# Two one-hots and two products of a step each in one VectorE instruction, the products behind the next step's one-hots

## Chip, cores and metric

One Trainium2 chip, one of its cores. The metric is the device time of the program in microseconds (us). The engines are PE (TensorE, with its weight loads as PEld), DVE (VectorE), ACT (ScalarE), POOL (GpSimd) and SP (SyncE, which issues DMAs).

## The reference, cut to what matters

One layer of a backbone over 1152 tokens (9 tiles of 128): modulation, a combined input projection, latent attention and retention, an output projection, and then an expert retrieval with product keys ("peer"). For each token and each of 8 heads the 16 best of 16384 = 128 x 128 experts are chosen; an expert's index is i * 128 + j.

```python
def peer(h, w_pq, sub_keys1, sub_keys2, u_table, v_table):
    ...
        cidx = (i1[..., :, None] * N_KEYS + i2[..., None, :]).reshape(PEER_BLOCK, PEER_HEADS, PEER_TOPK * PEER_TOPK)
        top_s, sel = lax.top_k(cand, PEER_TOPK)
        eidx = jnp.take_along_axis(cidx, sel, axis=-1)
        g = jax.nn.softmax(top_s, axis=-1).astype(xb.dtype)
        act = jax.nn.gelu(jnp.einsum('thkd,td->thk', u_table[eidx], xb), approximate=False)
        return jnp.einsum('thk,thkd->td', g * act, v_table[eidx])
```

## The kernel before, in words

The program is a row of stages with a barrier of all engines between them. Two of them matter here, `stage_weights` and the last, `stage_experts`.

The expert layer treats three of the nine token tiles sparsely (gathered rows of the tables) and six densely (768 tokens, in two groups of 384): there every expert's activation is computed for every token, and multiplied by that token's weight for that expert, which is zero for most. So for each dense token a 128 x 128 table of weights, W[i, j], is needed. It is made by a matmul: the partition is one of the token's 128 chosen (head, rank) pairs, the stationary operand is a one-hot of the pair's i over 128 keys, the moving one a one-hot of its j multiplied by the pair's share. The share is split into two float16 parts, so there are two matmuls a token, added in PSUM.

The class `WeightSteps` (L1705) holds this. A step covers B = 4 tokens; a group of 384 tokens has STEPS = 96 steps; a block of 16 tokens is stored to DRAM as a whole. Its methods:

- `vector` (L1734, DVE): a step's four instructions, all of 128 x 512 float16 (128 keys x 4 tokens). L1740 compares the key numbers (`iota`) with the pairs' j, giving `hot_j`; L1741 the same with i, giving `hot_i`; L1744 twice, `hot_j` times each part of the share, giving two `hot_w`. The buffers come in twos, by the parity `s` of the step. The columns of a step are four neighbouring tokens of the index (or share) table, repeated over the 128 keys by a stride of zero in the middle dimension; the four tokens are innermost and adjacent.
- `tensor` (L1747, PE): 8 matmuls of 128 x 128 (L1752) into a PSUM tile.
- `scalar` (L1756, ACT): evicts 128 x 512 values from PSUM (L1760).
- `store` (L1763, SP or POOL): writes a block to DRAM.

What orders a step are semaphores. `pw_full` starts at 2 (PE adds 2 at its start) and PE adds 1 at the end of each step. So DVE's wait for `pw_full >= n + 1` ahead of step n's first comparison means that the matmuls of step n - 2 are over; they were the last to read the buffers of that parity. `equal_full` counts the j comparisons, and the products wait for n + 1 of them. `hot_full` counts the finished products; PE waits for n + 1 ahead of step n. `pw_read` is what ACT has read (it starts at the number of PSUM buffers, here 2).

In `stage_weights` (L1770) the first group's 96 steps are made with nothing beside them. Ahead of the steps PE transposes the hidden rows of the three sparse tiles into `p_h` (L1825), and ACT reads them (L1835). `steps` unrolls the steps 0 and 1 and runs the others in a hardware loop (Fori) of two steps a turn, on DVE, PE and ACT alike. SP stores the 24 blocks.

In `stage_experts` (L1848) a group's 128 turns each go through one block of 128 experts: `down` and `up` matmuls of PE (L2124, L2125, L2128, L2144), the splits of the tables into two parts by ACT (L1976 `u_hi`, L1981 `v_hi`) and DVE (L2041 `u_lo`, L2048 `v_lo`), the activation by ACT (L1986) and, on DVE, the product with the weight (L2054) and its split (L2057, L2059), and the sparse tiles' three dot products or sums (L2066, L2079). In the first 96 turns of the first group the second group's weights are made on the way, one step a turn (`weights` in `blocks`): DVE's four instructions stand between `u_lo` and L2054, with their own buffers (named `next_`) and one PSUM buffer. DVE's part of this stage is written out, not looped.

One line elsewhere serves as a measure: L1640 (`stage_scores`) compares 16-bit values in a `tensor_tensor` of 128 x 2048, seen as 8 x 16 x 16 a partition, whose first operand is broadcast along the innermost dimension.

Of the kernel before, what the change touches and what calls it, by code (L numbers as in the profile page):

```python
# [10 lines left out]
F16 = mybir.dt.float16  # L11
ALU = mybir.AluOpType
# [3 lines left out]
P = 128  # L16
# [18 lines left out]
N_KEYS = 128  # L35
# [57 lines left out]
class Links:  # L93


    def __init__(self, eng, sem):
        self.eng, self.sem, self.base, self.n = eng, sem, 0, 0
# [939 lines left out]
def wait_count(eng, sem, count):  # L1037

    if not isinstance(count, int) or count > 0:
        eng.wait_ge(sem, count)  # L1040
# [664 lines left out]
class WeightSteps:  # L1705
# [5 lines left out]
    B = 4  # L1711
# [3 lines left out]
    def __init__(self, nc, sem, m, keep, banks, name, base, iota):  # L1715

        B = self.B
        self.nc, self.keep, self.banks, self.base = nc, keep, banks, base
        self.hot_i = [m.sb(f"{name}_hot_i{i}", [P, N_KEYS, B], F16) for i in range(2)]
        self.hot_j = [m.sb(f"{name}_hot_j{i}", [P, N_KEYS, B], F16) for i in range(2)]  # L1720
        self.hot_w = [[m.sb(f"{name}_hot_w{i}{k}", [P, N_KEYS, B], F16) for k in range(2)] for i in range(2)]
        self.iota = iota.rearrange("p (k b) -> p k b", b=B)
        self.wt = m.sb(f"{name}_wt", [P, 2, N_KEYS, BLOCK])
        self.pw = [m.ps(f"{name}_pw{i}", [P, B, N_KEYS]) for i in range(banks)]
        self.iota_full, self.equal_full, self.hot_full, self.pw_full, self.pw_read, self.wt_free, self.stored = (
            sem(f"{name}_{x}") for x in ("iota_full", "equal_full", "hot_full", "pw_full", "pw_read", "wt_free", "w_stored"))

    def keys(self, dve):
# [2 lines left out]
        self.nc.vector.tensor_copy(self.iota, src).then_inc(self.iota_full, 1)  # L1731
        dve.wait_ge(self.iota_full, 1)

    def vector(self, dve, n, s):  # L1734

        nc, keep = self.nc, self.keep
        shape = [P, N_KEYS, self.B]
        column = lambda x: x[:, bass.ds(n * self.B + self.base, self.B)].unsqueeze(1).to_broadcast(shape)
        dve.wait_ge(self.pw_full, n + 1)
        nc.vector.tensor_tensor(self.hot_j[s][:], self.iota, column(keep.index[:, 1]), ALU.is_equal).then_inc(self.equal_full, 1)  # L1740
        nc.vector.tensor_tensor(self.hot_i[s][:], self.iota, column(keep.index[:, 0]), ALU.is_equal)  # L1741
        dve.wait_ge(self.equal_full, n + 1)
        for k in range(2):
            last = nc.vector.tensor_tensor(self.hot_w[s][k][:], self.hot_j[s][:], column(keep.parts[:, k]), ALU.mult)  # L1744
        last.then_inc(self.hot_full, 1)

    def tensor(self, pe, n, s):  # L1747
        pe.wait_ge(self.hot_full, n + 1)
        pe.wait_ge(self.pw_read, n + 1)
        for b in range(self.B):  # L1750
            for k in range(2):
                last = self.nc.tensor.matmul(self.pw[s % self.banks][:, b, :], self.hot_i[s][:, :, b], self.hot_w[s][k][:, :, b],  # L1752
                                             start=k == 0, stop=k == 1)
        last.then_inc(self.pw_full, 1)

# [14 lines left out]
def stage_weights(nc, sem, m, keep, a):  # L1770

    iota = m.sb("iota", [P, N_KEYS * WeightSteps.B], F16)
    w = WeightSteps(nc, sem, m, keep, 2, "first", 0, iota[:])
    BLOCKS = w.STEPS // w.PER_BLOCK
    rest = m.sb("w_rest", [P, DENSE])
    hs = [m.sb(f"h_cols{s}", [P, KD, P]) for s in range(SPARSE)]
    p_idx = m.ps("p_idx", [P, 3, 512])
    p_h = m.ps("p_h", [P, KD, P])
    h_in = [sem(f"h_cols_in{s}") for s in range(SPARSE)]
    part_done, idx_full, idx_done, rows_full, rows_read = (  # L1780
        sem(x) for x in ("part_done", "idx_full", "idx_done", "h_rows_full", "h_rows_read"))

    def steps(eng, body):
        body(0, 0)
        body(1, 1)
        with eng.Fori(1, w.STEPS // 2) as k:
            for s in range(2):
                body(k * 2 + s, s)

    with nc.Block() as block:  # L1790

        @block.vector
        def _(dve):
            def link(ins, n):
                ins.then_inc(part_done, 1)
                dve.wait_ge(part_done, n)

            w.keys(dve)
            shares = keep.pairsT[:, 2, DENSE_AT:T]
            nc.vector.tensor_copy(keep.index, keep.pairsT[:, 0:2, DENSE_AT:T])  # L1800
            link(nc.vector.tensor_scalar(rest[:], shares, SHARE_UNIT, None, ALU.mult), 1)
            link(nc.vector.tensor_copy(keep.parts[:, 0, :], rest[:]), 2)
            link(nc.vector.tensor_sub(rest[:], rest[:], keep.parts[:, 0, :]), 3)
            link(nc.vector.tensor_copy(keep.parts[:, 1, :], rest[:]), 4)
            dve.wait_ge(idx_full, 1)
            tiles = lambda r: p_idx[:, r, 0:DENSE_AT].rearrange("p (s k) -> p s k", s=SPARSE)
            nc.vector.tensor_copy(keep.shares, tiles(2))
            nc.vector.tensor_copy(keep.dots, tiles(0)).then_inc(idx_done, 1)
            dve.wait_ge(idx_done, 1)
            nc.vector.scalar_tensor_tensor(out=keep.experts.bitcast(U32), in0=tiles(1), scalar=float(N_KEYS), in1=keep.dots,  # L1810
                                           op0=ALU.mult, op1=ALU.add).then_inc(idx_done, 1)
            steps(dve, lambda n, s: w.vector(dve, n, s))

        @block.tensor
        def _(pe):
            pe.sem_inc(w.pw_full, 2)
            for r in range(3):
                for s in range(SPARSE):
                    last = nc.tensor.transpose(p_idx[:, r, s * P:(s + 1) * P], keep.pairsT[:, r, s * P:(s + 1) * P], keep.ident)
            last.then_inc(idx_full, 1)  # L1820
            for s in range(SPARSE):
                pe.wait_ge(h_in[s], 16)
                wait_count(pe, rows_read, s)
                for k in range(KD):
                    last = nc.tensor.transpose(p_h[:, k, :], hs[s][:, k, :], keep.ident)  # L1825
                last.then_inc(rows_full, 1)
            steps(pe, lambda n, s: w.tensor(pe, n, s))

        @block.scalar
        def _(act):  # L1830
            act.sem_inc(w.wt_free, 1)
            act.sem_inc(w.pw_read, w.banks)
            for s in range(SPARSE):
                act.wait_ge(rows_full, s + 1)
                nc.scalar.activation(keep.h_rows[:, s, :], p_h[:].rearrange("p k c -> p (k c)"), ACT.Copy).then_inc(rows_read, 1)  # L1835
            steps(act, lambda n, s: w.scalar(act, n, s))

        @block.sync
        def _(sp):
            for s in range(SPARSE):  # L1840
                sp.dma_start(hs[s][:], keep.h2_dram[:, :, s * P:(s + 1) * P]).then_inc(h_in[s], 16)
            w.store(sp, 0)
            with sp.Fori(1, BLOCKS) as b:
                w.store(sp, b)
            sp.wait_ge(w.stored, 16 * BLOCKS)
# [430 lines left out]
```

## Time and profile before

| | us |
|---|---|
| median of 3 runs | 4201.07 (4199.33 to 4202.46) |
| the profiled execution | 4197.49 |
| its span, first to last instruction | 4195.7 |
| PE busy | 3802.9 (91%) |
| DVE busy | 2992.6 (71%) |
| ACT busy | 1232.7 (29%) |
| POOL busy | 1747.3 (42%) |
| mean granted PE clock | 0.932 |

The profile is one execution, taken by the hardware profiler. The steps of `stage_weights` run from about 1776 to 1917 us of the span; `stage_experts` begins at 1922 and ends with the kernel. A row of a timeline gives the start, the length, the engine, the line, the operation, output and inputs by the program's names, the shape and the number of instructions merged into the row; in brackets, how long the engine was idle before and whom it waited for. PEclk is the granted PE clock as a share of 2.4 GHz. A DVE instruction can begin before the one ahead of it has ended.

### The profile page before, as it was taken

How to read it: one execution, taken by the hardware profiler on the slowest of the kernel's cores; microseconds unless marked ns; L12 is line 12 of the kernel's file. 1: busy time of each engine (PE TensorE's matmuls, PEld its weight loads, DVE VectorE, ACT ScalarE, POOL GpSimd, SP SyncE). 2: the span in 40 equal slices, each digit the busy share in tenths (PEclk: the TensorE clock that was granted, in tenths of full speed). 3: DMA queues.
4: the chain of work that ended last, by engine and by line, in shares of the span. 5: the costliest groups of instructions: out<-in, count | busy, mean ns of one | idle time of the engine just before them, and what ended most of it. 6: DMA issues, size and time to landing. Idle time of an engine off the chain costs nothing.

```text
span 4195.7 us, 58772 instructions
## 1 busy us (share of the span) xinstructions
PE 3802.9 (91%) x19146; PEld 3082.0 (73%) x19146; DVE 2992.6 (71%) x6028; ACT 1232.7 (29%) x1871; POOL 1747.3 (42%) x1065
## 2 busy tenths in 40 slices
PE   8899876999668999387999999999989999999998
PEld 1699843566555444166999999999979999999997
DVE  0322244333441999897999999998888888888888
ACT  0411033222222222074333333333223232332332
POOL 0222000000220233202565565555557777777775
PEclk9799977899779999657999999999999999999999
DMA  7388700566433111047999999999999999999997
GB/s 248 114 269 286 250 2 20 161 202 205 139 111 97 35 35 35 15 180 278 328 339 333 327 339 327 346 327 354 336 336 338 343 333 345 336 341 345 331 347 273
DMA packets 302319, 1018.03 MB, mean 243 GB/s; under 512 B 30394, under 2 KB 61916, under 8 KB 294932
## 3 DMA queue, kind: packets, MB, share of 16 engines
q1 hardware_dynamic: 155348, 489.04, 34.8%
q0 software_dynamic: 127584, 481.35, 31.5%
q10 hardware_dynamic: 19296, 46.67, 2.9%
q8 instruction: 28, 0.46, 0.0%
q14 instruction: 63, 0.52, 0.0%
HBM read 875.22 MB, written 141.72 MB: 242 GB/s over the span
## 4 chain that ended last, share of the span: by engine, by line
PE 52%; DVE 1%; DMA 0%; issue 0%; ACT 0%; DVEq 0%; POOLq 0%
PE p_y L2144 25%; PE p_a L2125 9%; PE p_a L2124 9%; PE p_a L2128 8%; PE next_pw L1752 2%; DMA h_lo<-h_spill 0%; DVE p_y L2110 0%; DVE h_lo L2096 0%; DVE rows L2066 0%; DVE h_rows L2079 0%; DVE h_rows L2102 0%; DVE h_hi L2094 0%; DVE x1g L2113 0%; ACT pairsT L1986 0%; DVE u_raw L2105 0%
## 5 line engine op out<-in xcount | busy, mean ns | idle before, releaser
L2013 POOL DMA_INDIRECT rows<-in_v,pairsT x384 | 763.2, 1987 | 276.3 <-DVE h_rows L2079 184.4
L2013 POOL DMA_INDIRECT rows<-u_rows,pairsT x384 | 632.9, 1648 | 477.0 <-DVE pairsT L2066 404.5
L2124 PE MATMUL p_a<-h_hi,u_hi 128*128 128x384 f32 x2048 | 688.7, 336 | 39.3 <-DVE h_lo L2096 38.0
L2125 PE MATMUL p_a<-h_lo,u_hi 128*128 128x384 f32 x2048 | 692.1, 338 | 0.0
L2144 PE MATMUL p_y<-v_hi,g_hi 128*128 128x512 f32 x1536 | 486.9, 398 | 0.0
L1981 ACT ACTIVATE v_hi<-v_raw 128x1024 fp32r<-128x1024 f32 x256 | 272.0, 1062 | 727.0 <-PE p_y L2144 714.1
L2144 PE MATMUL p_y<-v_lo,g_hi 128*128 128x512 f32 x1536 | 475.8, 391 | 0.0
L2079 DVE SCALAR_TENSOR_TENSOR h_rows<-rows,pairsT,h_rows 128x1024 f32<-128x1024 f32 x381 | 466.4, 1279 | 2.1 <-DMA rows<-in_v,pairsT 2.1
L2066 DVE CUSTOM_DVE_ANT_0 rows<-rows,h_rows 128x1024 f32<-128x1024 f32 x384 | 450.6, 1220 | 24.1 <-DMA rows<-u_rows,pairsT 23.9
L2124 PEld LDWEIGHTS p_a<-h_hi,u_hi 128*128 128x128 f32 x2048 | 386.2, 189 | 50.4 <-DVE h_lo L2096 38.7
L2128 PE MATMUL p_a<-h_hi,u_lo 128*128 128x384 f32 x2048 | 396.8, 334 | 0.5 <-DVE u_lo L2041 0.5
L2125 PEld LDWEIGHTS p_a<-h_lo,u_hi 128*128 128x128 f32 x2048 | 385.9, 188 | 9.8
L2144 PE MATMUL p_y<-v_hi,g_lo 128*128 128x512 f32 x1536 | 389.7, 389 | 0.0
L2128 PEld LDWEIGHTS p_a<-h_hi,u_lo 128*128 128x128 f32 x2048 | 358.6, 188 | 0.8 <-DVE u_lo L2041 0.8
L2041 DVE TENSOR_TENSOR u_lo<-u_raw,u_hi 128x1024 fp32r<-128x1024 f32 x256 | 312.4, 1220 | 48.8 <-ACT u_hi L1976 47.5
L2144 PEld LDWEIGHTS p_y<-v_lo,g_hi 128*128 128x128 f32 x1536 | 288.3, 188 | 65.5
L2144 PEld LDWEIGHTS p_y<-v_hi,g_lo 128*128 128x128 f32 x1536 | 288.3, 188 | 59.9
L2144 PEld LDWEIGHTS p_y<-v_hi,g_hi 128*128 128x128 f32 x1536 | 281.0, 189 | 43.2
L2048 DVE TENSOR_TENSOR v_lo<-v_raw,v_hi 128x1024 fp32r<-128x1024 f32 x256 | 312.2, 1219 | 0.0
L1976 ACT ACTIVATE u_hi<-u_raw 128x1024 fp32r<-128x1024 f32 x256 | 270.1, 1055 | 14.8 <-DMA u_raw<-in_uT 14.8
L1478 PE MATMUL psc<-wc,hs 128*128 128x512 f32 x576 | 251.6, 595 | 0.0
L466 DVE COPY pairsT<-pT 128x1024 f32<-128x1024 f32 x64 | 78.3, 1224 | 232.8 <-DMA u_rows<-pairsT 143.6
(301 smaller groups left out, 5806.4 us busy)
## 6 DMA issues: line engine op xcount, KB each, us to landing
u_raw<-in_uT SPq DMA_DIRECT2D x256, 512.0 KB
v_raw<-in_v SPq DMA_DIRECT2D x256, 512.0 KB
w_ring<-weights_spill POOLq DMA_DIRECT2D x32, 1536.0 KB
u_rows<-pairsT ACTq DMA_DIRECT2D x64, 512.0 KB
key_cols<-in_uT SPq DMA_DIRECT2D x64, 512.0 KB, 4.1
u_rows<-key_rows SPq DMA_DIRECT2D x64, 512.0 KB
wada<-in_w_ada SPq DMA_DIRECT2D x12, 2048.0 KB, 7.9
weights_spill<-first_wt SPq DMA_DIRECT2D x24, 1024.0 KB
```

What stands on the lines that cost most here:

```text
L1478: last = nc.tensor.matmul(psc[:, 4 * b:4 * b + 4, :], hs[:, k, :], wc[:, k, 4 * b:4 * b + 4, :], start=k == 0, stop=k == KD - 1)
L1976: nc.scalar.activation(u_hi[s][:], u_raw[s][:], ACT.Copy).then_inc(uhi_full, 1)
L1981: nc.scalar.activation(v_hi[s][:], v_raw[s][:], ACT.Copy).then_inc(vhi_full, 1)
L2013: pool.indirect_dma_start(rows[s][n % SLOTS][:], None, (keep.u_rows, v_rows)[g], at).then_inc(rows_in[s][n % SLOTS], 16)
L2041: nc.vector.tensor_sub(u_lo[s][:], u_raw[s][:], u_hi[s][:].bitcast(F32)).then_inc(ulo_full, 1)
L2048: nc.vector.tensor_sub(v_lo[s][:], v_raw[s][:], v_hi[s][:].bitcast(F32)).then_inc(vlo_full, 1)
L2066: nc.vector.tensor_tensor_reduce(out=slot[:], in0=slot[:], in1=keep.h_rows[:, s, :], op0=ALU.mult, op1=ALU.add, scale=1.0, scalar=0.0, acc ...
L2079: nc.vector.scalar_tensor_tensor(out=total, in0=slot[:], scalar=share, in1=total, op0=ALU.mult, op1=ALU.add).then_inc(rows_used, 1)
L2124: nc.tensor.matmul(p_a[:, 0:GT], u_hi[s][:, k, :], h_hi[:, k, :], start=k == 0, stop=False)
L2125: nc.tensor.matmul(p_a[:, 0:GT], u_hi[s][:, k, :], h_lo[:, k, :], start=False, stop=False)
L2128: last = nc.tensor.matmul(p_a[:, 0:GT], u_lo[s][:, k, :], h_hi[:, k, :], start=False, stop=k == KD - 1)
L2144: last = nc.tensor.matmul(p_y[i][:, half, :], part, vv[:, half * 512:(half + 1) * 512], start=first and hi and vv is v_hi[s], stop=end and ...
```

## The change

The two one-hots (i and j) become one tile `hot` of 128 x 2 x 128 x 4 float16, and the two products one tile `hot_w` of the same shape, each made by one instruction over 1024 elements a partition. `vector` is split into `equal` and `weighted`. `stage_experts` still calls `vector`, which issues the one behind the other. In `stage_weights` DVE's order is now: the one-hots of step n + 1, then the products of step n. The counts of the waits are the same functions of the step's number as before. PE's, ACT's and SP's code is the same but for the operands' names.

```diff
-        self.hot_i = [m.sb(f"{name}_hot_i{i}", [P, N_KEYS, B], F16) for i in range(2)]
-        self.hot_j = [m.sb(f"{name}_hot_j{i}", [P, N_KEYS, B], F16) for i in range(2)]
-        self.hot_w = [[m.sb(f"{name}_hot_w{i}{k}", [P, N_KEYS, B], F16) for k in range(2)] for i in range(2)]
+        self.hot = [m.sb(f"{name}_hot{i}", [P, 2, N_KEYS, B], F16) for i in range(2)]
+        self.hot_w = [m.sb(f"{name}_hot_w{i}", [P, 2, N_KEYS, B], F16) for i in range(2)]
...
+    def columns(self, x, n):
+
+        return x[:, :, bass.ds(n * self.B + self.base, self.B)].unsqueeze(2).to_broadcast([P, 2, N_KEYS, self.B])
+
+    def equal(self, dve, n, s):
+
+        dve.wait_ge(self.pw_full, n + 1)
+        keys = self.iota.unsqueeze(1).to_broadcast([P, 2, N_KEYS, self.B])
+        self.nc.vector.tensor_tensor(self.hot[s][:], keys, self.columns(self.keep.index, n), ALU.is_equal).then_inc(self.equal_full, 1)
+
+    def weighted(self, dve, n, s):
+
+        dve.wait_ge(self.equal_full, n + 1)
+        hot_j = self.hot[s][:, 1].unsqueeze(1).to_broadcast([P, 2, N_KEYS, self.B])
+        self.nc.vector.tensor_tensor(self.hot_w[s][:], hot_j, self.columns(self.keep.parts, n), ALU.mult).then_inc(self.hot_full, 1)
+
     def vector(self, dve, n, s):
...
-        dve.wait_ge(self.pw_full, n + 1)
-        nc.vector.tensor_tensor(self.hot_j[s][:], self.iota, column(keep.index[:, 1]), ALU.is_equal).then_inc(self.equal_full, 1)
-        nc.vector.tensor_tensor(self.hot_i[s][:], self.iota, column(keep.index[:, 0]), ALU.is_equal)
-        dve.wait_ge(self.equal_full, n + 1)
-        for k in range(2):
-            last = nc.vector.tensor_tensor(self.hot_w[s][k][:], self.hot_j[s][:], column(keep.parts[:, k]), ALU.mult)
-        last.then_inc(self.hot_full, 1)
+        self.equal(dve, n, s)
+        self.weighted(dve, n, s)
...
-                last = self.nc.tensor.matmul(self.pw[s % self.banks][:, b, :], self.hot_i[s][:, :, b], self.hot_w[s][k][:, :, b],
+                last = self.nc.tensor.matmul(self.pw[s % self.banks][:, b, :], self.hot[s][:, 0, :, b], self.hot_w[s][:, k, :, b],
...
-            steps(dve, lambda n, s: w.vector(dve, n, s))
+            def step(n, s):
+                w.equal(dve, n + 1, 1 - s)
+                w.weighted(dve, n, s)
+
+            w.equal(dve, 0, 0)
+            step(0, 0)
+            step(1, 1)
+            with dve.Fori(1, w.STEPS // 2 - 1) as k:
+                for s in range(2):
+                    step(k * 2 + s, s)
+            step(w.STEPS - 2, 0)
+            w.weighted(dve, w.STEPS - 1, 1)
```

## Rows read from the trace of the kernel before

**Rows 1.** The page: busy time of each engine.
```profile
PE 3802.9 (91%) x19146; PEld 3082.0 (73%) x19146; DVE 2992.6 (71%) x6028; ACT 1232.7 (29%) x1871; POOL 1747.3 (42%) x1065
```

**Rows 2.** Windows of the weights stage and of the expert stage; columns on top.
```profile
core 0: us, PE busy (x) PEld busy (x) DVE busy (x) ACT busy (x) POOL busy (x), PEclk, DMA share, GB/s
...
1800.00:1900.00 100.00, 80.56 (x582) 60.30 (x583) 100.00 (x291) 78.14 (x73) 0.00 (x0) 0.50 0.46 189
...
1948.00:2840.00 892.00, 892.00 (x4826) 806.42 (x4825) 826.21 (x1441) 324.66 (x383) 517.36 (x325) 1.00 0.93 332
```

**Rows 3.** Timeline of the weights stage's first steps.
```profile
1783.09 1.99 PEld L1752 LDWEIGHTS first_pw<-first_hot_w,first_hot_i 128*128 128x128 f16 x16
1783.30 2.07 PE L1752 MATMUL first_pw<-first_hot_w,first_hot_i 128*128 128x128 f16 x16
...
1784.60 0.43 DVE L1740 TENSOR_TENSOR first_hot_j<-iota,gate 128x512 f16<-128x512 f16 x1 [5.56 <-PE first_pw L1752]
...
1786.09 1.11 PE L1752 MATMUL first_pw<-first_hot_w,first_hot_i 128*128 128x128 f16 x8 [0.72 <-DVE first_hot_w L1744]
...
1787.36 0.42 DVE L1740 TENSOR_TENSOR first_hot_j<-iota,gate 128x512 f16<-128x512 f16 x1
1787.43 1.11 PE L1752 MATMUL first_pw<-first_hot_w,first_hot_i 128*128 128x128 f16 x8 [0.23 <-DVE first_hot_w L1744]
...
1787.70 0.42 DVE L1741 TENSOR_TENSOR first_hot_i<-iota,gate 128x512 f16<-128x512 f16 x1
1788.04 0.75 DVE L1744 TENSOR_TENSOR first_hot_w<-first_hot_j,gate 128x512 f16<-128x512 f16 x2
1788.71 0.43 DVE L1740 TENSOR_TENSOR first_hot_j<-iota,gate 128x512 f16<-128x512 f16 x1
...
1788.85 1.12 PE L1752 MATMUL first_pw<-first_hot_w,first_hot_i 128*128 128x128 f16 x8 [0.30 <-DVE first_hot_w L1744]
```

**Rows 4.** Timeline of the weights stage's last steps and the next stage's start.
```profile
1911.73 1.11 PE L1752 MATMUL first_pw<-first_hot_w,first_hot_i 128*128 128x128 f16 x8 [0.26 <-DVE first_hot_w L1744]
...
1913.00 0.42 DVE L1740 TENSOR_TENSOR first_hot_j<-iota,gate 128x512 f16<-128x512 f16 x1
...
1914.49 1.12 PE L1752 MATMUL first_pw<-first_hot_w,first_hot_i 128*128 128x128 f16 x8 [0.26 <-DVE first_hot_w L1744]
...
1921.98 0.35 SPq L1938 DMA_DIRECT2D u_raw<-in_uT  x1
```

**Rows 5.** Groups of DVE and ACT instructions, 1786 to 1913.
```profile
L1744 DVE TENSOR_TENSOR first_hot_w<-first_hot_j,gate 128x512 f16<-128x512 f16 x185 | 69.6, 417 | 0.0
L1740 DVE TENSOR_TENSOR first_hot_j<-iota,gate 128x512 f16<-128x512 f16 x92 | 39.0, 424 | 0.0
...
L1760 ACT ACTIVATE first_wt<-first_pw 128x512 f32 (+1 forms) x92 | 99.1, 1077 | 28.3 <-PE first_pw L1752 21.8 <-SPq L1765 3.4 <-issue 3.2
```

**Rows 6.** Instructions of line 1740: the register work ahead of the comparison.
```profile
L1740 DVEq FUSED_REGOPS  x94: 75/75/81, 1784.5 to 1912.9; - x94
```

**Rows 7.** Timeline of DVE in one weighted turn of the expert stage.
```profile
2056.97 1.22 DVE L2041 TENSOR_TENSOR u_lo<-u_raw,u_hi 128x1024 fp32r<-128x1024 f32 x1
2058.11 0.42 DVE L1740 TENSOR_TENSOR next_hot_j<-pairsT,gate 128x512 f16<-128x512 f16 x1
...
2059.45 0.55 DVE L2054 TENSOR_TENSOR pairsT<-pairsT,w_ring 128x384 f32<-128x384 f32 x1
2060.04 0.36 DVE L2057 CAST g_hi<-pairsT 128x384 fp32r<-128x384 f32 x1
```

**Rows 8.** Waits between 1948 and 2840: us in total, times, longest.
```profile
DVE u_lo L2041 <- ACT u_hi L1976: 42.5, 69, 0.7
```

**Rows 9.** Groups of DVE instructions, whole span: another 16-bit tensor_tensor with a broadcast.
```profile
L1640 DVE TENSOR_TENSOR mix<-sel_abf,starts 128x2048 bf16<-128x2048 bf16 x9 | 20.6, 2292 | 0.3
L1640 DVE TENSOR_TENSOR mix<-sel_abf,iota 128x2048 bf16<-128x2048 bf16 x9 | 20.6, 2284 | 0.0
```

More of the change, by code:

```diff
@@ L1732, in keys @@
         dve.wait_ge(self.iota_full, 1)
-    def vector(self, dve, n, s):
-        nc, keep = self.nc, self.keep
-        shape = [P, N_KEYS, self.B]
-        column = lambda x: x[:, bass.ds(n * self.B + self.base, self.B)].unsqueeze(1).to_broadcast(shape)
-        dve.wait_ge(self.pw_full, n + 1)
-        nc.vector.tensor_tensor(self.hot_j[s][:], self.iota, column(keep.index[:, 1]), ALU.is_equal).then_inc(self.equal_full, 1)
-        nc.vector.tensor_tensor(self.hot_i[s][:], self.iota, column(keep.index[:, 0]), ALU.is_equal)
-        dve.wait_ge(self.equal_full, n + 1)
-        for k in range(2):
-            last = nc.vector.tensor_tensor(self.hot_w[s][k][:], self.hot_j[s][:], column(keep.parts[:, k]), ALU.mult)
-        last.then_inc(self.hot_full, 1)
+    def columns(self, x, n):
[8 more added lines that the diff above has]
+        self.nc.vector.tensor_tensor(self.hot_w[s][:], hot_j, self.columns(self.keep.parts, n), ALU.mult).then_inc(self.hot_full, 1)
+    def vector(self, dve, n, s):
+        self.equal(dve, n, s)
+        self.weighted(dve, n, s)
     def tensor(self, pe, n, s):
```

## The prediction

> **What bounds the kernel now.** I read the page first, to see how much of the span belongs to the code touched, then each of the two stages that use it, by windows, by groups of instructions and as a timeline. The page says that PE is busy 91% and DVE 71% [rows 1]. That is a mean over stages. The windows part two stages from each other [rows 2]: in the expert stage (1948 to 2840, while it still makes weights) PE has no idle time at the full clock; in the weights stage (1800 to 1900) DVE reads 100.00 of 100 us, PE 80.56 and ACT 78.14, at a granted clock of 0.50, the 1.2 GHz level.
>
> *The weights stage.* DVE at 100% looks like a DVE bound, and the change looks like fewer instructions for the bound engine. The timeline says more. Call the n-th group of matmuls PE(n). PE(2) starts at 1786.09 and the equality of step 4 at 1787.36; PE(93) starts at 1911.73 and the equality of step 95 at 1913.00: 1.27 us both times [rows 3, 4]. Step 5's is at 1788.71, 1.28 after PE(3) at 1787.43. Never earlier, at either end of the stage. So the wait on `pw_full` is binding: each equality starts when PE has finished the step two before (1.11 us of matmuls, then some 0.16 for the semaphore and DVE's 75 ns of register work [rows 6]). From the first equality of a step to the end of its last product is 0.68 + 0.75 = 1.43 us (1787.36, 1788.04, length 0.75), and PE starts 0.06 later (1788.79 to 1788.85) [rows 3]. The loop PE(n-2), DVE(n), PE(n) is 1.275 + 1.43 + 0.06 = 2.765 us and spans two steps: 1.382 a step. Measured: from step 2's equality at 1784.60 to step 95's at 1913.00, 128.40 / 93 = 1.381. The instructions of 417 to 424 ns start every 0.33 us and so overlap [rows 3, 5], which is why a loop through a semaphore shows as a DVE without idle time. Two loops interleave, one for even steps and one for odd; DVE needs 4 x 0.333 = 1.33 itself, almost as much.
>
> *The expert stage.* A weighted turn takes about 9.25 us, PE filled. DVE is busy 826.21 of 892 us, so has 65.8 / 96 = 0.69 us a turn to spare [rows 2], and waits 42.5 us there for ACT's `u_hi` [rows 8].
>
> **The change, part by part.**
>
> *1. Two instructions for four.* A 16-bit 128x512 lasts 0.417 and starts 0.333 after the one before [rows 3, 5]; a 32-bit 128x1024 lasts 1.22 and is followed 1.14 later (2056.97, 2058.11) [rows 7]. Against the 0.55 of 384 elements (L2054) [rows 7] the latter gives (1.22 - 0.55) / 640 = 1.05 ns an element and a fixed 0.15 of length. Taking the same 0.15 off 0.417 leaves 0.267 for 512 elements, 0.52 ns each, and so 0.067 fixed between starts. So 1024 16-bit elements at the present pace cost 0.533 + 0.067 = 0.60 between starts and 0.683 in length (estimates). Bounds: between starts at least 0.53 (no fixed part), at most 0.667 (nothing saved); length 0.62 to 0.75 (the pair now). I take 0.60 and 0.683. Gain on DVE alone: 1.333 - 1.20 = 0.13 us a step.
>
> The far bound is another pace altogether. L1640, a 16-bit tensor_tensor of 2048 with a broadcast operand and more dimensions, lasts 2284 to 2292 ns, twice our time per element [rows 9]. There the broadcast repeats one element innermost; here the innermost run remains four neighbouring tokens, as it is now, and only an outer dimension of 2 is added, so I take the fast pace. The Trainium skill has the rule, in "VectorE: DVE Perf Modes", What auto-detection actually checks: two results a cycle if every tensor is 16-bit with innermost step 1. By that rule too the merged instruction keeps the pace, and L1640 agrees with it.
>
> *2. The order.* This is the term that matters. The semaphore starts at 2 and PE(n) makes it n + 3. The equality of step m waits for m + 1, hence for PE(m-2). Before, what stood ahead of it on DVE was the products of m-1, and PE(m-2) needs only those of m-2: one whole step of slack. Now `step(n)` issues the equality of m = n + 1 and then the products of n. The equality of n + 1 waits for PE(n-1), which waits for the products of n-1, **the instruction directly ahead of that equality on DVE**. Queued behind the waiting equality are the products of n, for which PE(n) waits. So nothing overlaps any more: products(n-1), PE(n-1), equality(n+1), products(n), PE(n). One period is now one step:
> 1.275 (start of PE(n-1) to the equality) + 0.60 (to the products) + 0.683 (their length) + 0.06 (to PE(n)) = 2.62 us.
> The wait of the products for their own equality is met long before and costs nothing; the cover is the other equality and a whole PE step.
>
> *3. The stage.* PE(0) is held until 1783.09 by the transposes of `p_h`, not by DVE, and stays at 1783.30 [rows 3]. Equality 2 stays at 1784.60; the products of step 1 are now behind it and end at 1784.60 + 0.60 + 0.68 = 1785.88; PE(1) at 1785.94. PE(94) 93 periods later: 1785.94 + 93 x 2.62 = 2029.6. The last products wait for nothing, so PE(95) follows after a plain PE step, at least 7 x 0.117 and about 1.0: 2030.6. Before it was at 1914.49 [rows 4]. Difference: **+116 us**. ACT's step (1.08 us) and the stores of four steps' results each fit into 2.62 and 10.5 us; from the last matmul to the next stage at 1921.98 is as before. The clock is at 0.50 already [rows 2], and a PE with more idle time has no lower level to fall to.
>
> *4. The expert stage.* Here `vector` is the equality and the products with nothing between. The products now wait for an instruction just issued. The nearest row: L2054, 0.55 long, is followed by its dependent L2057 after 0.59 (2059.45, 2060.04) [rows 7], so a dependent start costs the length plus 0.04. DVE's step: 0.683 + 0.04 + 0.60 = 1.32 against 1.34 now (2058.11 to 2059.45). Even were the gap 0.2 us longer, the 0.69 of slack a turn covers it, and PE sets the end: 0. If that cover were gone, each 0.1 us would cost 96 x 0.1 = 9.6 us.
>
> *Sum.* The profiled execution's 4197.5 us becomes 4313.5. It lies 3.6 below the median of the runs, 4201.07; on that scale: **4317 us**, 2.8% slower.
> Bounds: a period of 1.27 + 0.53 + 0.62 + 0.05 = 2.47 gives 93 x 2.47 - 127.5 = +102; 1.28 + 0.667 + 0.75 + 0.06 = 2.76 gives +129. That is 4303 to 4330, and some us either way for what else shifts.
>
> **The rivals.**
>
> *A. The merged instructions lose the fast pace.* Against it: the innermost run is unchanged. For it: L1640 shows that such an instruction can run at half the pace. Then between starts 1.14, length 1.22: period 1.275 + 1.14 + 1.22 + 0.06 = 3.70, and 93 x 1.08 = 100 us more. In the expert stage DVE's step would be 1.26 + 1.14 = 2.40, 1.06 over now, 0.37 over the slack, so DVE would set the turn: 96 x 0.37 = 36 us. Together 4317 + 100 + 36 = 4453. If only one of the two loses it, about half.
>
> *B. Faster: the wait does not bite and the saved fixed costs remain.* It would need equality n + 1 to be released by PE(n-2), at the place of the `pw_full` wait in the loop. Then DVE alone sets the step, at 1.20: 93 x (1.20 - 1.381) = -17 us, 4184. It decides as soon as PE's answer returns within the 0.60 us of one products instruction; the rows say 1.27, and it starts only when they are done, so it cannot. The Trainium skill speaks for this side: "VectorE: DVE Perf Modes", Rules for kernel authors, advises to keep the number of DVE operations small rather than that of semaphores, since the flush behind each one comes anyway. The fixed 0.067 us of fixed time between starts bears that out for DVE alone; that rule looks at one engine, and would turn this forecast's sign.
>
> *C. No change: the added wait is absorbed by a stall that I do not see*, so that the merged pair and the lost overlap cancel. There is no idle time of 1.2 us a step anywhere in rows 2 to 5 to absorb it. 4201.
>
> **How the numbers follow.** The forecast has 0.90: the count of the semaphore is plain in the code and the loop's latency is a row at both ends of the stage. A has 0.06, B 0.03, C 0.01. What a measurement of this kernel tells from no change is about 0.2%, 8.4 us. Slower is forecast and A, 0.96; faster is B, 0.03; same C, 0.01. The rivals lie far from the forecast and hold 0.10, so the range stays with the forecast's own bounds, 4303 to 4330, widened a little for the scatter of runs (3 us) and for second-order shifts: 4300 to 4336.
>
> **What would show it.** In the profile after: the weights stage ends near 2038 in place of 1922; DVE has two groups of 96 instructions of about 0.68 us there, and idle time of about 1.3 us ahead of each equality, put down to PE `first_pw`; PE idle about 1.5 us a step, put down to DVE; PE(n) starts 2.6 us apart; busy DVE in 1800 to 1900 falls from 100% to about 50%. The expert stage keeps its 9.25 us turns and its length. Wrong would be: instructions of 1.2 us (A), periods near 1.2 to 1.4 us with no idle DVE (B), or an expert stage longer by over 5 us, which would mean that DVE's slack there was not the cover I take it for.

## The result and the profile after

The changed kernel takes 4315.77 us (median of 4 runs, 4312.65 to 4318.72) against 4201.76 before it on the same chip: a ratio of 1.0272, 95% interval 1.0254 to 1.029, so slower by 114 us. The profiled execution has a span of 4312.6 us, 116.9 more than the one before. Forecast were 4317 us and a range of 4300 to 4336.

Busy time of the engines, from the page:

```profile
PE 3802.1 (88%) x19146; PEld 3082.3 (71%) x19146; DVE 2979.8 (69%) x5644; ACT 1231.0 (29%) x1871; POOL 1735.1 (40%) x1065
```

No engine works noticeably more than in [rows 1] (PE's weight loads 0.3 us); DVE has 384 instructions and 12.8 us less. The added time is idle time. The windows say where; the first lies in the weights stage, the second is the expert stage's weighted part, moved by 116 us (columns on top):

```profile
core 0: us, PE busy (x) PEld busy (x) DVE busy (x) ACT busy (x) POOL busy (x), PEclk, DMA share, GB/s
...
1800.00:1900.00 100.00, 42.63 (x310) 31.97 (x309) 49.16 (x76) 40.10 (x38) 0.00 (x0) 0.50 0.23 94
...
2064.00:2956.00 892.00, 892.00 (x4826) 806.50 (x4825) 822.87 (x1249) 324.82 (x383) 518.08 (x324) 1.00 0.94 332
```

Against [rows 2], the expert stage is the same to the matmul: 4826 in 892 us, PE without a gap. In the weights stage 310 matmuls pass in 100 us where 582 did, and DVE falls from 100.00 to 49.16. Its timeline, the first steps and the last:

```profile
1784.14 1.13 PE L1759 MATMUL first_pw<-first_hot_w,first_hot 128*128 128x128 f16 x8
...
1785.31 0.69 DVE L1741 TENSOR_TENSOR first_hot<-iota,gate 128x1024 f16<-128x1024 f16 x1 [6.31 <-PE first_pw L1759]
...
1786.66 1.11 PE L1759 MATMUL first_pw<-first_hot_w,first_hot 128*128 128x128 f16 x8 [1.39 <-DVE first_hot_w L1747]
...
1787.94 0.69 DVE L1741 TENSOR_TENSOR first_hot<-iota,gate 128x1024 f16<-128x1024 f16 x1 [1.34 <-PE first_pw L1759]
1788.55 0.68 DVE L1747 TENSOR_TENSOR first_hot_w<-first_hot,gate 128x1024 f16<-128x1024 f16 x1
1789.29 0.83 PEld L1759 LDWEIGHTS first_pw<-first_hot_w,first_hot 128*128 128x128 f16 x8 [1.80 <-DVE first_hot_w L1747]
...
2030.32 2.06 PE L1759 MATMUL first_pw<-first_hot_w,first_hot 128*128 128x128 f16 x16 [1.39 <-DVE first_hot_w L1747]
...
2038.73 0.35 SPq L1956 DMA_DIRECT2D u_raw<-in_uT  x1
```

This is to be read in turns. PE(1) starts at 1786.66, the one-hots at 1787.94 (1.28 later), the products at 1788.55, PE(2) at 1789.29. DVE is idle for 1.34 us while PE works, and PE for about 1.5 while DVE works: "PE waits for DVE" and "DVE waits for PE" of similar size, in the same stretch, on the same pair of tiles, is the mark of a loop that is closed once a step. In [rows 3, 4] the same loop ran over two steps; once the stage was under way (from PE(3) on), DVE showed no wait there and PE one of 0.23 to 0.30 us. PE(94) starts at 2030.32, so the period is (2030.32 - 1786.66) / 93 = 2.620 us.

The waits between 1790 and 2030 (total, times, longest):

```profile
PE first_pw L1759 <- DVE first_hot_w L1747: 137.4, 91, 1.5
DVE first_hot L1741 <- PE first_pw L1759: 122.0, 92, 1.3
```

DVE in a weighted turn of the expert stage:

```profile
2173.35 0.68 DVE L1741 TENSOR_TENSOR next_hot<-pairsT,gate 128x1024 f16<-128x1024 f16 x1
2174.07 0.69 DVE L1747 TENSOR_TENSOR next_hot_w<-next_hot,gate 128x1024 f16<-128x1024 f16 x1
2174.68 0.55 DVE L2072 TENSOR_TENSOR pairsT<-pairsT,w_ring 128x384 f32<-128x384 f32 x1
```

The step takes 1.33 us, where it was 1.34 [rows 7]. From the stage's first DMA to the end are 4312.6 - 2038.73 = 2273.9 us; before, 4195.7 - 1921.98 = 2273.7.

### The profile page after: what moved, and what is told of

It is laid out like the page before. It is cut to its first block, busy times and chain, and to the rows that moved or that the text cites. A ratio compares the mean times of both kernels' runs of the same rounds, so it can differ in the third digit from the quotient of the medians.

```text
span 4312.6 us, 58192 instructions
## 1 busy us (share of the span) xinstructions
PE 3802.1 (88%) x19146; PEld 3082.3 (71%) x19146; DVE 2979.8 (69%) x5644; ACT 1231.0 (29%) x1871; POOL 1735.1 (40%) x1065
## 4 chain that ended last, share of the span: by engine, by line
PE 50%; DVE 1%; DMA 1%; issue 0%; POOL 0%; ACT 0%; ACTq 0%; DVEq 0%; POOLq 0%
PE p_y L2162 23%; PE p_a L2143 8%; PE p_a L2142 8%; PE p_a L2146 8%; PE next_pw L1759 2%; DMA rows<-u_rows,pairsT 1%; DMA h_lo<-h_spill 0%; DVE rows L2084 0%; DVE p_y L2128 0%; DVE h_lo L2114 0%; DVE h_rows L2097 0%; POOL rows L2031 0%; DVE h_rows L2120 0%; DVE h_hi L2112 0%; DVE x1g L2131 0%
## 5 line engine op out<-in xcount | busy, mean ns | idle before, releaser
L2031 POOL DMA_INDIRECT rows<-in_v,pairsT x384 | 750.3, 1954 | 288.2 <-DVE h_rows L2097 199.9
L2066 DVE TENSOR_TENSOR v_lo<-v_raw,v_hi 128x1024 fp32r<-128x1024 f32 x256 | 312.3, 1220 | 0.0
```

What stands on the lines that cost most here:

```text
L2031: pool.indirect_dma_start(rows[s][n % SLOTS][:], None, (keep.u_rows, v_rows)[g], at).then_inc(rows_in[s][n % SLOTS], 16)
L2066: nc.vector.tensor_sub(v_lo[s][:], v_raw[s][:], v_hi[s][:].bitcast(F32)).then_inc(vlo_full, 1)
```

## The experiments

The experiments ran on three chips, each beside the kernel before on the same chip (medians 4200.4, 4201.1 and 4201.2 us), to which the ratios refer. The total moves by a few us from run to run, so beside it stands a finer measure from the traces: the time from the first to the last weight load of PE in the weights stage. For the changed kernel (number: minimum/median/maximum length in ns, first and last start in us), and for the fastest version below:

```profile
L1759 PEld LDWEIGHTS first_pw<-first_hot_w,first_hot x768: 111/126/151, 1783.9 to 2032.0; 128*128 128x128 f16 x192
```

```profile
L1761 PEld LDWEIGHTS first_pw<-first_hot_w,first_hot x768: 111/125/151, 1784.5 to 1898.5; 128*128 128x128 f16 x192
```

| kernel | first to last load, us | median, us | ratio to before (95%) |
|---|---|---|---|
| before | 1783.1 to 1915.2: 132.1 | 4201 | |
| the change | 248.1 | 4315.8 | 1.0254 to 1.029 |
| merge only | 1783.9 to 1921.4: 137.5 | 4204.6 | 1.0000 to 1.0018 |
| order only | 1781.7 to 2043.5: 261.8 | 4330.6 | 1.0296 to 1.0328 |
| three one-hot buffers | 1788.4 to 1915.8: 127.4 | 4195.8 | 0.998 to 0.9998 |
| 4 one-hot, 3 product, 3 PSUM buffers | 114.0 | 4182.0 | 0.9941 to 0.9968 |
| the same, not merged | 1785.6 to 1912.2: 126.6 | 4196.0 | 0.9979 to 0.9997 |
| merge only, DVE written out | 1789.5 to 1917.2: 127.7 | 4195.7 | 0.9979 to 0.9997 |
| the change, DVE written out | 1784.4 to 2021.3: 236.9 | 4305.1 | 1.0237 to 1.0268 |
| the change, half of the stage's matmuls | 1784.9 to 1987.7: 202.8 | 4269.6 | 1.0148 to 1.0182 |
| before, half of the stage's matmuls | 1784.6 to 1912.1: 127.5 | 4195.0 | 0.9977 to 0.9997 |
| the change, one more comparison a weighted turn | 1782.9 to 2030.9: 248.0 | 4318.5 | 1.0264 to 1.0298 |
| the same, one token broadcast innermost | 1783.0 to 2031.0: 248.0 | 4366.2 | 1.038 to 1.0415 |

**Merge or order?** Two runs take the change apart. The first keeps the merged instructions and the old order:

```diff
-            w.equal(dve, 0, 0)
-            step(0, 0)
...
+            steps(dve, lambda n, s: w.vector(dve, n, s))
```

> The merged instructions in the old order: equality and products of step n, nothing between, also in the weights stage. Theory (the order is the cause, the merge costs nothing): the equality again follows PE(n-2). From its start to the end of the products 0.72 + 0.69 = 1.41 us (the merged rows of the changed kernel's expert stage: 2173.35, 2174.07), so two steps take 1.275 + 1.41 + 0.06 = 2.745 and one 1.37, against 1.381: about 1 us less in all, 4201 within 3 us. Rival (the merge is the cause, since PE must wait for one large product and the products for one large comparison): most of the 114 us stays, above 4260.

The second keeps the order and splits both instructions again:

```diff
+        for r in (1, 0):
+            at = self.keep.index[:, r, bass.ds(n * self.B + self.base, self.B)].unsqueeze(1).to_broadcast(shape)
+            last = self.nc.vector.tensor_tensor(self.hot[s][:, r], self.iota, at, ALU.is_equal)
...
+        for k in range(2):
...
+            last = self.nc.vector.tensor_tensor(self.hot_w[s][:, k], self.hot[s][:, 1], at, ALU.mult)
```

> The new order with four separate instructions of 512 elements (two comparisons, two products). Theory: the loop through PE is closed once a step, with DVE's part 1.43 us as in the kernel before: 1.275 + 1.43 + 0.06 = 2.765 us a step, 0.145 more than the changed kernel's 2.62, so 93 x 0.145 = 13 us above its 4316: 4329. Rival (the merge is the cause): near 4201.

Measured 4204.6 and 4330.6. The order is the cause: alone it costs 130 us, with the merge 114. The rival (above 4260, and near 4201) is out by 55 us in the one run and by 130 in the other. The order alone shows the same turns with a longer part of DVE: PE to PE 2.78 us, and the comparisons 1.30 after PE:

```profile
1851.01 1.12 PE L1765 MATMUL first_pw<-first_hot_w,first_hot 128*128 128x128 f16 x8 [1.65 <-DVE first_hot_w L1752]
1852.31 0.76 DVE L1743 TENSOR_TENSOR first_hot<-iota,gate 128x512 f16<-128x512 f16 x2 [1.36 <-PE first_pw L1765]
...
1853.79 1.11 PE L1765 MATMUL first_pw<-first_hot_w,first_hot 128*128 128x128 f16 x8 [1.67 <-DVE first_hot_w L1752]
```

But the merge alone is no gain either, 4 us worse where 1 better was expected. On the total alone that is barely told from no change (the interval begins at 1.0000); the stage says it more clearly, 137.5 us for 132.1. Its timeline:

```profile
1850.11 0.68 DVE L1741 TENSOR_TENSOR first_hot<-iota,gate 128x1024 f16<-128x1024 f16 x1
...
1850.25 1.11 PE L1759 MATMUL first_pw<-first_hot_w,first_hot 128*128 128x128 f16 x8 [0.32 <-DVE first_hot_w L1747]
...
1850.93 0.69 DVE L1747 TENSOR_TENSOR first_hot_w<-first_hot,gate 128x1024 f16<-128x1024 f16 x1
1851.54 0.69 DVE L1741 TENSOR_TENSOR first_hot<-iota,gate 128x1024 f16<-128x1024 f16 x1
```

The products start 0.82 us after their one-hots, not 0.72 as in the expert stage, whose DVE code is written out. DVE's own time is then 0.82 + 0.61 = 1.43 us a step, more than the 1.38 of the kernel before, and the saving of two instructions is gone. (The loop through PE over two steps has the gap in it too and gives nearly the same, (1.27 + 0.82 + 0.69 + 0.06) / 2 = 1.42.) With four small instructions another comparison, that of i, stood between the comparison of j and the products; with two large ones nothing stands there.

**Is that gap register work of the loop?** The same kernel, DVE's 96 steps written out:

```diff
-            steps(dve, lambda n, s: w.vector(dve, n, s))
+            for n in range(w.STEPS):
+                w.vector(dve, n, n % 2)
```

> The merged instructions in the old order, with DVE's 96 steps written out in place of its hardware loop (PE's and ACT's loops stay). In the looped version the products began 0.82 us after their one-hots, not 0.72, and DVE's own 0.82 + 0.61 = 1.43 us set the step. Theory: the 0.10 is register work that DVE's queue does only once the wait of the products is met, and it is gone here: DVE 0.72 + 0.61 = 1.33 us, the loop of two steps 1.20 + 1.41 + 0.06 = 2.67, so 1.34 a step, 93 x 0.10 = 9 us less than the looped version: 4196. Rival (the gap belongs to the dependent pair whatever the code around it): as the looped version, 4204.

```profile
1850.87 0.69 DVE L1741 TENSOR_TENSOR first_hot<-iota,gate 128x1024 f16<-128x1024 f16 x1
...
1851.60 0.69 DVE L1747 TENSOR_TENSOR first_hot_w<-first_hot,gate 128x1024 f16<-128x1024 f16 x1
1852.21 0.69 DVE L1741 TENSOR_TENSOR first_hot<-iota,gate 128x1024 f16<-128x1024 f16 x1
```

0.73 us, 1.34 a step, 4195.7: as expected. The unmerged kernel with DVE written out was not run, so how much of the 5 us under the kernel before is the merge's, and how much that of writing out, stays open. In the looped version this row (operation, times: min/median/max in ns) stands between the two, register work of DVE's queue that comes only when the wait is met (the last one-hots run from 1919.1 to 1919.8, this starts at 1919.8, the products at 1919.9). It is 0.06 of the 0.09 us; the rest is not resolved:

```profile
L1747 DVEq FUSED_REGOPS  x94: 57/57/57, 1786.2 to 1919.8; - x94
```

The changed kernel, written out in the same way (its `step` called for n from 0 to 94 in place of the loop):

> The changed kernel with DVE's steps of the weights stage written out. Theory: the answer of PE comes back as late as before, less the 57 to 75 ns of register work ahead of the one-hots: 2.62 - 0.07 = 2.55 us a step, 93 x 0.07 = 7 us less: 4309. The serial loop stays. Rival (what costs is the hardware loop on DVE): far less than 4290.

```profile
1852.12 1.11 PE L1759 MATMUL first_pw<-first_hot_w,first_hot 128*128 128x128 f16 x8 [1.39 <-DVE first_hot_w L1747]
1853.27 0.69 DVE L1741 TENSOR_TENSOR first_hot<-iota,gate 128x1024 f16<-128x1024 f16 x1 [1.21 <-PE first_pw L1759]
```

Measured 4305.1, 10.7 us less rather than 7. PE(n-1) to the one-hots are now 1.15 us in place of 1.27, so the loop form had cost 0.12 there, 0.07 of it the register row and the rest not resolved. The hardware loop adds to the serial period; it is not what makes it serial.

**Is PE's time wholly exposed?** Half of the weights stage's matmuls, those of the share's low part, are left out, in the changed kernel and in the one before:

```diff
+        parts = 1 if self.banks == 2 else 2
         for b in range(self.B):
-            for k in range(2):
+            for k in range(parts):
```

> The changed kernel with the second of each token's two matmuls left out in the weights stage (the share's low part is missing there). Theory: PE's step is wholly exposed in the loop, so a step of 4 matmuls less at 0.117 us each is 0.47 shorter, 2.15 us: 94 x 0.47 = 44 us off 4316, 4272. Rival (DVE or a store sets the step): no change, 4316.

> The kernel before with the same matmuls left out (the share's low part is missing in the weights stage). Theory: the loop over two steps shortens to 2.30 us, 1.15 a step, and DVE's four instructions take over at 1.33 to 1.36: 93 x 0.02 to 0.05 = 2 to 4 us off, about 4198. Were PE exposed as in the changed kernel, it would be 44 off; were DVE alone the bound, nothing.

Measured 4269.6 and 4195.0. The same 4 matmuls a step are worth 46 us in the changed kernel (first to last load 202.8 for 248.1) and 6 in the one before (127.5 for 132.1, its DVE at 1.34 us a step). In the order of before, PE's work lay beside DVE's; in the new one it is added to it.

**Do more buffers mend it?** A third one-hot buffer, with loops of six steps, lets the one-hots of n + 1 wait for PE(n-2):

```diff
-        dve.wait_ge(self.pw_full, n + 1)
+        s = s % self.hots
+        wait_count(dve, self.pw_full, n + 3 - self.hots)
```

> The change with a third buffer for the one-hots in the weights stage (loops of 6 steps a turn), so that the one-hots of step n + 1 wait for PE(n-2), as they did before the change. Theory: two steps a loop, 1.275 + 0.61 + 0.68 + 0.06 = 2.63 us, 1.31 a step, 93 x 0.07 = 6 us under the kernel before: 4195. The PSUM loop (1.46 from PE's start to ACT's, 1.07, back to PE) gives 1.29 a step, just under it. Rival (something else in the merged order costs time, the wait is only where it shows): stays above 4260.

> Four buffers for the one-hots, three for the products, three PSUM buffers in the weights stage (loops of 12 steps): the one-hots of n + 1 wait for PE(n-3). Theory: no loop through PE binds any more (three steps for 2.63 us) and DVE's own two instructions set the step, 0.61 + 0.61 = 1.22 us: 93 x 0.16 = 15 us under the kernel before, 4186. If ACT's eviction (1.07 and its wait) sets it instead: 1.30 or so a step, 4194.

> The version with four one-hot, three product and three PSUM buffers, in the new order, but with four separate instructions a step. It parts that version's 18 us into buffers and merge. Theory: no loop through PE binds, DVE's four instructions set the step at 1.33 us: 93 x 0.05 = 4 us under the kernel before, 4196, so that 4 come from the buffers and 13 from the merge, which only now is on the path. Rival (all of it is the buffers): 4182.

All three landed near their numbers: 4195.8, 4182.0 and 4196.0. The deeper set is 4 us under its number. With the third buffer, the order that cost 114 us costs nothing; the step is 127.4 / 95 = 1.34 us rather than 1.31. The longer loop turns that came with the buffer are not what undid it: with all steps written out and two buffers the change still takes 4305.1. The rows read as if ACT's way back bound beside DVE's:

```profile
1850.91 0.85 PEld L1761 LDWEIGHTS first_pw<-first_hot_w,first_hot 128*128 128x128 f16 x8 [0.43 <-DVE first_hot_w L1749]
...
1852.39 1.08 ACT L1769 ACTIVATE first_wt<-first_pw 128x512 f32 x1 [0.20 <-SPq L1774]
1852.80 0.68 DVE L1749 TENSOR_TENSOR first_hot_w<-first_hot,gate 128x1024 f16<-128x1024 f16 x1
...
1853.59 0.85 PEld L1761 LDWEIGHTS first_pw<-first_hot_w,first_hot 128*128 128x128 f16 x8 [0.44 <-DVE first_hot_w L1749]
```

ACT evicts the PE step of 1850.91 from 1852.39 to 1853.47, and PE's next load into that PSUM buffer is at 1853.59: a loop of 2.68 us over two steps, 1.34 a step. The products end at 1853.48, within 0.01 of ACT, and the profile puts PE's wait down to them. No run changes the PSUM buffers alone, so this cause is read and not shown. With the deeper set DVE waits for nobody (1800 to 1890) and goes without a gap at 0.60 us an instruction:

```profile
1879.82 0.68 DVE L1743 TENSOR_TENSOR first_hot<-iota,gate 128x1024 f16<-128x1024 f16 x1
1880.42 0.68 DVE L1749 TENSOR_TENSOR first_hot_w<-first_hot,gate 128x1024 f16<-128x1024 f16 x1
1881.03 0.68 DVE L1743 TENSOR_TENSOR first_hot<-iota,gate 128x1024 f16<-128x1024 f16 x1
```

Here the merge pays: unmerged, the same buffers give 126.6 us of stage, merged 114.0, 12.6 / 95 = 0.13 us a step, the figure that the saved fixed parts give. (In the serial loop the merge took 14 us off the stage too, 261.8 to 248.1, since there all of DVE's time counts; but that stage is twice as long.) Three kinds of buffers and the length of the loops' turns changed together here, and no run parts them. The deeper merged version is 18 us faster than the kernel before and 134 faster than the changed one.

**Is the expert stage's slack what it was taken for?** One more comparison a weighted turn, into a tile of its own, in the fast form and then with one token broadcast innermost:

```diff
...
+        at = self.keep.index[:, :, bass.ds(n * self.B + self.base, self.B)].unsqueeze(2).to_broadcast(whole)
+        self.nc.vector.tensor_tensor(self.extra[:], self.iota.unsqueeze(1).to_broadcast(whole), at, ALU.is_equal)
```

> The changed kernel with one more comparison of 1024 16-bit elements in each weighted turn of the expert stage (into a tile of its own): 0.61 us more for DVE, 96 times. Theory: DVE's slack there, (892 - 822.9) / 96 = 0.72 us a turn, still hides it: 4316 to 4320. Rival (DVE sets that stage's turn): 96 x 0.61 = 58 more, 4374.

> The same with the additional comparison's second operand broadcast innermost too (one token for all). Theory: that takes the slow pace of the kernel's other 16-bit comparison with such a broadcast, 1.22 us long, 1.14 between starts, 0.42 over the slack: 96 x 0.42 = 40 us more, 4356. If the pace stays at 0.61: as the run before it. If the slack is not what the windows say: between 4316 and 4426.

Measured 4318.5 and 4366.2. The added group of each, in turn:

```profile
L1755 DVE TENSOR_TENSOR next_extra<-pairsT,gate 128x1024 f16<-128x1024 f16 x96 | 66.0, 687 | 0.0
```

```profile
L1755 DVE TENSOR_TENSOR next_extra<-pairsT,gate 128x1024 f16<-128x1024 f16 x96 | 117.1, 1220 | 0.0
```

and two of the second one's waits between 2064 and 2956:

```profile
PEld next_pw L1764 <- DVE next_hot_w L1748: 44.8, 87, 0.6
PE next_pw L1764 <- DVE next_hot_w L1748: 17.3, 85, 0.3
```

The first is hidden whole (first to last `next_pw` load 879.1 us, as before). The second is not: 923.7 us, 44.7 more or 0.47 a turn, and PE now waits for the products. So 1.14 - 0.47 = 0.67 us a turn can be used, close to the 0.69 and 0.72 that the windows give; the total of 50 is 10 over what was expected, about half of it in these turns (44.7 for 40), the rest outside them and not explained. The two forms differ in one stride, and in length by 687 to 1220 ns.

## Why the prediction was right

- *The binding wait.* That the equality is always 1.27 to 1.28 us behind PE(n-2) was read as a loop at a time when DVE showed 100% busy. The pair with half of the matmuls bears it out from the other side: take PE's work away in the kernel before, and it goes to DVE's 1.34 us and no further.
- *Part 1, the two large instructions.* 0.60 between starts and 0.683 long were estimated; 0.61 and 0.684 to 0.692 measured. The fast pace holds with the additional outer dimension, so rival A is out. That a broadcast along the innermost dimension would have about halved it is shown by the second of the runs with an added comparison. The rule of the Trainium skill that the prediction cites ("VectorE: DVE Perf Modes", What auto-detection actually checks: two results a cycle if every tensor is 16-bit with innermost step 1) is borne out on both sides, 687 and 1220 ns.
- *Part 2, the order.* 2.62 us a step forecast, 2.620 measured. The pair of merge alone and order alone shows that the cause is the order, and the third buffer that it is the wait's distance within the order.
- *Part 3, the stage.* +116 forecast, +116.0 between first and last load, 116.9 in the span and 114 in the medians. Two small things that the sum left out offset each other on the scale of the runs: PE(0) came at 1784.14, 0.84 later than before through something in an earlier stage, and the profiled execution lay 1.4 us below its median, not 3.6. That part of the closeness is luck.
- *Part 4, the expert stage.* 1.32 forecast, 1.33 measured, hidden; the cover of 0.69 us a turn was 0.67.
- *Rival B, and the rule that spoke for it.* The advice of the Trainium skill to keep the count of VectorE operations small ("VectorE: DVE Perf Modes", Rules for kernel authors) is good for 0.13 us a step where nothing but DVE binds, as the two deep versions show. In the old order with the old buffers it brought nothing (merge only, 4204.6), and with the new order it came along with a loss nine times its size. What the prediction passed over, in what the merge alone is worth, is that it takes away the instruction that had stood between a one-hot and its product; in the loop this costs 0.13 us, from the end of the one to the start of the other, and the new order was a cure for that, at a price of 1.24 us a step.

## What to carry to other kernels

Before an instruction is moved ahead of another on a queue, count for its wait which step of the other engine it needs, and which instruction of its own queue that step needs; if that is the instruction directly ahead, the two engines take turns. Work that is moved one step ahead needs one more buffer. An engine that reads 100% busy can still be paced by a semaphore: look for a constant distance between another engine's start and its own, at both ends of the stage, and count over how many steps the loop closes.

## What the runs showed of the hardware that was not expected

- In a hardware loop, an instruction that waits for the one just ahead of it starts 0.13 us after that one's end (0.82 for 0.69); written out with constants, 0.04 (0.73). The register row of 57 ns is part of the difference; the rest is not resolved. The answer of PE to DVE comes 0.12 us sooner when written out (1.15 for 1.27).
- The length of an instruction is not its price. In the kernel before with half of the matmuls, the same 128x512 comparisons are 485 ns long in place of 417 to 424, and still start every 0.33 us. Why they are longer stays open.
- In the deepest version, with PE busy 18.39 of 20 us (1840 to 1860), the granted clock is 0.57, where it is 0.50 throughout the stage in the kernel before, so part of the time it is at the higher level. It changes nothing, since DVE sets the step (columns as in the windows above):

```profile
1840.00:1860.00 20.00, 18.39 (x135) 13.73 (x134) 20.00 (x35) 17.87 (x18) 0.00 (x0) 0.57 0.54 223
```
